# Norm phases that accumulate three projections chunk by chunk, and phases handed over without a meeting of all engines

## Chip, cores and metric

One core of one Trainium2 chip. The metric is the device time of one launch in microseconds (us), here the median of three runs; below, TensorE, VectorE, ScalarE, GpSimd and SyncE are the core's five engines. TensorE multiplies, the three in the middle work elementwise, SyncE only issues the DMA transfers.

## What is computed

One inference step of a trunk of two layers with a final norm. There are 1088 tokens (1024 of a new stream, 64 of a running one), 1024 features, all in fp32. In each layer:

```
mod = silu(c) @ ada_w + ada_b                 # shift, scale, gate of 1024 each, for two kinds of token
h = rmsnorm(x, norm_w) * (1.0 + scale) + shift
proj = h @ w_in                               # q, k, v, z of retention; q, k, v, f, z of fox;
                                              # q, k, v, a, b, z of delta; merge gates
logf = log_sigmoid(ff + fox_f_bias)           # fox: cumulated over the tokens, subtracted in the scores
g = -exp(gdn_a_log) * softplus(ga + gdn_dt_bias);  beta = sigmoid(gb)
o_r = retention(rotary(q), rotary(k), v)      # 4 heads, chunks of 64
o_f = softmax(q k + fcum_q - fcum_k) v        # fox: 8 heads, causal
o_g = gated_delta_rule(l2norm(q), l2norm(k), v, g, beta)   # 4 heads, chunks of 64
br = [rmsnorm(o_r)*silu(z), o_f*silu(z), rmsnorm(o_g)*silu(z)] @ w_branch
x = x + gate * (sum(br * sigmoid(merge gates)) @ w_out)
```

The columns called ff, ga and gb (16 of them in all) are "the gates" of this document. Beside the two outputs of the trunk the step returns the new states of all three branches.

## The kernel before

**Layout.** Features lie on the 128 partitions in eight chunks (`KC`), tokens along the free dimension in three segments of 364, 364 and 360 (`SEGS`). A full fp32 product is made of three fp32r products, high by high, high by low and low by high (`three`, L251 to L256); so h and every block of weights (1024 x 128) exist as a high and a low part. SyncE loads blocks ahead into six raw slots. GpSimd splits each with a cast and a subtraction (`split_block`, L304 to L311). Two split blocks fit in `sb_w_split`. Of h, ScalarE rounds the high part.

**Phases.** The launch is a row of 25 phases: per layer the norm, two retention groups, four fox groups, four delta groups and the merge; then the final norm. Each phase is a program block of its own with one instruction list per engine. At its end `barrier()` (L226) lets all engines meet and clears all semaphores of phases, so that each phase counts from zero; only the counters of loaded and split weight blocks run through the launch.

**Fillers.** Inside a phase TensorE's list is written out by hand. Between the steps of a recurrence or of scores it turns the projections of that group: `blocks` yields one "turn" at a time, which is one chunk of one segment, three matmuls, some 0.5 us; a block has 24 turns. `turns(fill, n)` takes n of them, and the numbers (`front_turns`, the 4 and 8 in retention, 25 at the start of fox) are what covers the other engines' work at that place. A block's last turn releases a PSUM bank to ScalarE, which copies it out.

**The norm phase** (`norm_phase`, L381). x comes in four transfers. ScalarE squares a chunk, TensorE adds the squares over partitions with a matrix of ones (L479), ScalarE takes logarithm and exponential (L518, L521) for the inverse root. Then VectorE multiplies all eight chunks of x with it (L588). Chunk by chunk, ScalarE scales with 1 + scale times the norm's weight, adds the shift and rounds (L550, the high part of h); VectorE forms the difference to the rounded one (L607) and it or ScalarE (L616, L537) the low part. TensorE takes the gates' block as chunks appear: segment 0 over all chunks, then segments 1 and 2. Query and key of retention's first group follow as whole blocks. VectorE turns the gates' rows into logf, g and beta with two scans along the tokens (L645, L647), and SyncE stores them for the later phases. In layer 0 the modulation of a pair of chunks is first computed: TensorE multiplies c with blocks of ada_w (L365), ScalarE copies the row (L527), TensorE turns it into columns (L372), VectorE adds the bias (L378).

**Retention, fox, delta.** Retention starts with five half-swaps for the rotary (L721), projects V for nine bank entries, and waits for the rotated q and k (L745 scores of pairs, L755 transposes). Fox starts with 25 turns and ScalarE's copies of q and k (L1149); the mask that its scores need is prepared by GpSimd (L1060) from a row that SyncE broadcasts. Delta starts with 24 turns, sums of squares for k and q (L335) with ScalarE's logarithms behind them (L1573), and then the products between keys (L1417, L1424).

## Time and profile before

| | |
|---|---|
| median of 3 runs | 3165.54 us (3164.61 to 3170.79) |
| the profiled execution | 3164.03 us |
| its span | 3162.3 us |
| mean granted clock of TensorE | 0.978 |
| TensorE busy | 2948.4 us, 93% |
| VectorE, ScalarE, GpSimd busy | 1106.3, 1014.3, 801.0 us (35%, 32%, 25%) |
| moved by DMA | 269.39 MB, 85 GB/s on average |

The span runs from the first to the last instruction that the profiler recorded. The page cuts it into 40 slices of 79 us and gives each the busy tenths of an engine:

```profile
PE   5999999999999999999959999999999999999996
DVE  3312233233433433155143212343334433422632
PEclk7999999999999999999969999999999999999998
```

PE is TensorE's matmuls, DVE is VectorE, PEclk is the clock that TensorE was granted, in tenths of the full one. Slice 1 holds layer 0's norm, slice 21 layer 1's, slice 40 the final one. In the views of waits an engine with a small q behind it (PEq) is its sequencer.

### The profile page before, as it was taken

To read this page: it belongs to the slowest core of one execution; us is meant where nothing else is said; L and a number is where in the kernel's file an instruction comes from. 1 tells how busy PE (TensorE), PEld (TensorE's weight loads), DVE (VectorE), ACT (ScalarE), POOL (GpSimd) and SP (SyncE) were. 2 spreads that over 40 slices of the span, in tenths; PEclk is the share of its full clock that TensorE was granted. 3 is DMA by queue.
4 is the path that set the end of the run, shared out by engine and by line. 5 is a ranking of instruction groups with operands and counts; after the bars stand their busy time and mean duration, and the time that the engine had idled before them with its cause. 6 is when DMAs were issued, how large, how long until landed. Compare 5 with 4: busy or idle time off the path is not lost. (4 is left out here: it accounts for less than half of the span.)

```text
span 3162.3 us, 55678 instructions
## 1 busy us (share of the span) xinstructions
PE 2948.4 (93%) x24012; PEld 2686.5 (85%) x24012; DVE 1106.3 (35%) x2568; ACT 1014.3 (32%) x1822; POOL 801.0 (25%) x520
## 2 busy tenths in 40 slices
PE   5999999999999999999959999999999999999996
PEld 3988888888898898999948888888888898899995
DVE  3312233233433433155143212343334433422632
ACT  4121423323434544222041214233325534531201
POOL 0221212212313323332212122212213313333320
PEclk7999999999999999999969999999999999999998
DMA  5111223223212211253222112212212211123323
GB/s 217 61 55 49 105 93 116 105 87 115 74 54 56 60 47 56 92 178 101 92 104 68 69 36 90 88 44 90 84 43 57 66 47 56 60 86 142 129 98 142
DMA packets 109956, 269.39 MB, mean 85 GB/s; under 512 B 38992, under 2 KB 45264, under 8 KB 108688
## 3 DMA queue, kind: packets, MB, share of 16 engines
q1 hardware_dynamic: 109712, 265.83, 24.8%
q8 instruction: 190, 3.11, 0.4%
q14 instruction: 54, 0.44, 0.1%
HBM read 208.20 MB, written 57.60 MB: 84 GB/s over the span
## 5 line engine op out<-in xcount | busy, mean ns | idle before, releaser
L254 PE MATMUL ps<-sb_h_split,sb_w_split 128*128 128x364 f32 (+1 forms) x3312 | 1180.7, 356 | 76.8 <-PEq L227 29.6
L256 PE MATMUL ps<-sb_h_split,sb_w_split 128*128 128x364 f32 (+1 forms) x3312 | 1092.7, 330 | 0.1
L255 PE MATMUL ps<-sb_h_split,sb_w_split 128*128 128x364 f32 (+1 forms) x3312 | 1092.6, 330 | 0.0
L254 PEld LDWEIGHTS ps<-sb_h_split,sb_w_split 128*128 128x128 f32 x3312 | 629.8, 190 | 145.4 <-issue 90.0
L308 POOL CAST sb_w_split<-sb_w_raw 128x1024 fp32r<-128x1024 f32 x154 | 166.4, 1081 | 1957.5 <-PE ps L256 1614.0
L255 PEld LDWEIGHTS ps<-sb_h_split,sb_w_split 128*128 128x128 f32 x3312 | 630.3, 190 | 6.4
L256 PEld LDWEIGHTS ps<-sb_h_split,sb_w_split 128*128 128x128 f32 x3312 | 627.4, 189 | 0.4 <-issue 0.4
L310 POOL TENSOR_TENSOR sb_w_split<-sb_w_raw,sb_w_split 128x1024 fp32r<-128x1024 f32 x154 | 370.5, 2406 | 12.3
L1230 DVE COPY sb_fox<-ps 128x512 f32<-128x512 f32 (+3 forms) x208 | 109.0, 541 | 290.4 <-PE ps L1112 289.9
L296 ACT ACTIVATE sb_raw_qk<-ps 128x364 f32<-128x364 f32 (+2 forms) x176 | 64.5, 393 | 347.0 <-PE ps L256 347.0
L1171 ACT ACTIVATE sb_fox<-sb_fox 128x128 f32<-128x128 f32 (+5 forms) x144 | 111.2, 773 | 98.2 <-DVE sb_fox L1208 98.0
L290 ACT ACTIVATE sb_fox<-ps 128x364 f32<-128x364 f32 (+1 forms) x96 | 45.5, 474 | 300.8 <-PE ps L256 300.8
L255 PE MATMUL ps<-sb_h_split,sb_wb_split 128*128 128x364 f32 (+1 forms) x384 | 125.9, 328 | 0.0
L256 PE MATMUL ps<-sb_h_split,sb_wb_split 128*128 128x364 f32 (+1 forms) x384 | 125.6, 327 | 0.0
L254 PE MATMUL ps<-sb_h_split,sb_wb_split 128*128 128x364 f32 (+1 forms) x384 | 125.4, 327 | 0.0
L1112 PE MATMUL ps<-sb_masks,sb_fox 128*128 128x128 f32 (+1 forms) x656 | 105.8, 268 | 0.0
L1202 DVE CUSTOM_DVE_ANT_0 sb_fox<-ps,sb_fox 128x128 f32<-128x128 f32 x144 | 39.9, 277 | 170.3 <-PE ps L1078 126.4
L1112 PEld LDWEIGHTS ps<-sb_masks,sb_fox 128*128 128x128 f32 (+1 forms) x656 | 80.0, 139 | 14.8 <-issue 7.4
L1078 PE MATMUL ps<-sb_fox 64*128 64x512 f32 (+3 forms) x448 | 88.8, 503 | 0.0
L1198 DVE CUSTOM_DVE_ANT_0 sb_fox<-ps,sb_fox 128x256 f32<-128x256 f32 (+7 forms) x128 | 86.3, 674 | 0.0
L1123 PE MATMUL ps<-sb_fox 128*64 128x128 f32 (+2 forms) x1312 | 84.6, 272 | 1.7 <-DVE sb_fox L1230 1.5
L1123 PEld LDWEIGHTS ps<-sb_fox 128*64 128x64 f32 (+1 forms) x1312 | 68.0, 136 | 19.5 <-issue 11.1
(263 smaller groups left out, 4332.0 us busy)
## 6 DMA issues: line engine op xcount, KB each, us to landing
sb_w_raw<-in_wblk SPq DMA_DIRECT2D x154, 512.0 KB, 5.5
sb_ada_fox<-in_adaw SPq DMA_DIRECT2D x32, 512.0 KB, 4.3
sb_raw_qk<-scratch_gate SPq DMA_DIRECT2D x24, 544.0 KB, 3.7
sb_fox<-scratch_fcum SPq DMA_DIRECT2D x8, 1600.0 KB, 7.2
sb_w_raw<-in_wbr SPq DMA_DIRECT2D x48, 256.0 KB, 4.2
scratch_gate<-sb_fox SPq DMA_DIRECT2D x16, 544.0 KB
scratch_gate<-sb_delta SPq DMA_DIRECT2D x16, 544.0 KB
sb_h_split<-scratch_o SPq DMA_DIRECT2D x16, 544.0 KB, 10.5
```

The source lines that it names most:

```text
L254: pe.matmul(out, w_hi, x_hi, start=first, stop=False)
L255: pe.matmul(out, w_hi, x_lo, start=False, stop=False)
L256: return pe.matmul(out, w_lo, x_hi, start=False, stop=last)
L296: ins = act.activation(buf[:, u:u + w], ps[:, first_bank + e % banks, c:c + w], ACT.Copy)
L308: pool.tensor_copy(ws[:, to, 0], wraw[:, slot]).then_inc(split_hi, 1)
L310: pool.tensor_tensor(ws[:, to, 1], wraw[:, slot], ws[:, to, 0].bitcast(F32), ALU.subtract)\
L1078: mm = pe.matmul(ps[0:rows, 2 * h + a // 512, 0:w], qT[64 * h:64 * h + 64, P * t:P * t + rows], kT[64 * h:64 * h + 64, lo + a:lo + a + w], ...
L1112: mm = pe.transpose(ps[0:w, b, P * j:P * j + rows], lg[0:rows, h, (c + j) * P:(c + j) * P + w], ident[0:rows, 0:rows])
L1123: pe.matmul(ps[64 * h:64 * h + 64, b, 0:rows], V[0:w, vt, 64 * h:64 * h + 64], PT[0:w, h, P * c:P * c + rows], start=(c == 0), stop=(c == ...
L1171: act.activation(lg[0:rows, h, 0:n], lg[0:rows, h, 0:n], ACT.Exp, bias=mx[0:rows, s, 2:3], accum_out=mx[0:rows, s, 3:4])\
L1198: dve.tensor_tensor_reduce(out=lg[0:rows, h, 0:n], in0=src[:, 0:n], in1=fk[0:rows, h, lo:lo + n], scale=0.125, scalar=-3e38, op0=ALU.subtr ...
L1230: ins = dve.tensor_copy(dst[:, 0:full, 0:rows], src[:, 0:full, 0:rows])
```

## The change

**Handing over.** The semaphores of phases exist twice, as two sets; phases use them in turn, so a phase needs no cleared counters at its start. All phases stand in one program block. Each engine ends a phase with `leave`, which raises its own counter `done[...]`. ScalarE, VectorE, GpSimd and SyncE begin the next with `enter`: they wait for the other four counters. GpSimd then clears the set of the phase before. TensorE doesn't wait there; it waits for ScalarE alone after eight turns (fox, delta), or before the fourth half-swap (retention's second groups), and at the end of a phase for the copies of its own banks.

```
+        def enter(eng, me, nr):
+            if nr >= 2:
+                eng.wait_ge(sets_cleared, nr - 1)
+            if nr >= 1 and me != "pe":
+                for who in done:
+                    if who != me:
+                        eng.wait_ge(done[who], nr)
+            if nr >= 1 and me == "pool":
+                eng.sem_clear(clears[(nr - 1) % 2])
+                eng.sem_inc(sets_cleared, 1)
+        def leave(eng, me):
+            if me == "pe":
+                eng.sem_inc(done[me], 1)
+            else:
+                eng.drain().then_inc(done[me], 1)
...
-        def barrier():
-            nc.multi_engine_barrier(list(nc.engines), sems_to_clear=clear)
...
+        both = [phases_of(half) for half in range(2)]
+        with nc.Block() as block:
+            for nr, (p, what) in enumerate(order):
+                with ExitStack() as ph:
+                    both[nr % 2][p](block, *what, ph, nr)
```

**The norm.** The gates' weights get a buffer of their own. Gates, query and (in layer 1) two of key's three segments are accumulated side by side in all eight PSUM banks, chunk by chunk; the rest of key follows. In layer 1 the factors 1 + scale times weight are formed at the start and GpSimd multiplies them into x while the squares are summed. VectorE normalises a chunk and forms the low part in one operation. In layer 0 the modulation's products and turns stand between the chunks.

```
+                    def scale_x(k):
+                        pool.wait_ge(squares, k + 1)
+                        for c, (a, w) in enumerate(KINDS):
+                            ins = pool.tensor_scalar(x[:, k, a:a + w], x[:, k, a:a + w], scw[:, k, c:c + 1], None,
+                                                     ALU.mult)
+                        ins.then_inc(merged, 1)
+                    if not first_layer:
+                        pool.wait_ge(scaled, 2)
+                        for k in range(4):
+                            scale_x(k)
+                    split_block(pool, L, 0, wx)
+                    if not first_layer:
+                        for k in range(4, KC):
+                            scale_x(k)
                     split_block(pool, L, 1)
...
+                    def products(k):
+                        if first_layer:
+                            pe.wait_ge(*((level_x, k // 2 + 1) if k % 2 else (h_ready, k // 2 + 1)))
+                        else:
+                            pe.wait_ge(h_ready, k + 1)
+                        for what, s in early:
+                            if k == 0 and s == 0:
+                                await_split(pe, L, what)
+                            product(what, s, k)
...
+                    for k in range(KC):
+                        products(k)
+                        if first_layer and k % 2 == 0 and k < 6:
+                            turn_mods(k // 2 + 1)
+                        if first_layer and k in (1, 3):
+                            mods(k // 2 + 2)
...
+                        normalise(0)
+                        for k in range(KC):
+                            if k + 1 < KC:
+                                normalise(k + 1)
+                            dve.wait_ge(h_hi, k + 1)
+                            for c, (a, w) in enumerate(KINDS):
+                                ins = dve.scalar_tensor_tensor(hs[:, 1, k, a:a + w], x[:, k, a:a + w],
+                                                               modT[:, L, k, c:c + 1],
+                                                               hs[:, 0, k, a:a + w].bitcast(F32),
+                                                               ALU.add, ALU.subtract)
+                            ins.then_inc(h_ready, 1)
```

In the gates' tail, two memsets go to GpSimd, a copy and a scaling to ScalarE, ScalarE's copies of query and key (in layer 1 all six, in layer 0 three) come before its part of the tail, and the scan for g stands before the one for the cumulated logf, whose row is now stored last.

**Fillers.** The split of a retention group's second block moves into the phase before. Retention's 4 turns after each pair of scores go, and the three gaps of 8 turns become 12; in first groups the sixth half-swap stands behind V's fourth entry. In delta the three sums for q are cut in two, with four turns before the last, and ScalarE takes one bank entry earlier. Fox of layer 0 gets 8 turns before its modulation rows.

```
-            front_turns = [24, 4, 10, 2, 4]
+            front_turns = [24, 12, 12, 2, 4]
...
-                    turns(fill, front_turns[0])
+                    turns(fill, 8)
+                    pe.wait_ge(done["act"], nr)
+                    turns(fill, front_turns[0] - 8)
                     pe.wait_ge(squares, 1)
                     sum_features(pe, ring, 0, sq[1])
                     turns(fill, front_turns[1])
                     pe.wait_ge(squares, 2)
-                    sum_features(pe, ring, 3, sq[0])
-                    turns(fill, front_turns[2])
+                    sum_features(pe, ring, 3, sq[0], range(2))
+                    turns(fill, 4)
+                    sum_features(pe, ring, 3, sq[0], range(2, 3))
+                    turns(fill, front_turns[2] - 4)
```

**How rows move on the engines.** The first place is TensorE in layer 1's norm, behind the last sum of squares. `sb_w_split` is the pair of split weight blocks, `sb_h_split` is h. Before:

```order
L479 MATMUL ps<-sb_norm_layer1,sb_masks 128x360
L254 MATMUL ps<-sb_h_split,sb_w_split 128x364 [waits h_ready,roots,split_ready]
L255 MATMUL ps<-sb_h_split,sb_w_split 128x364
L256 MATMUL ps<-sb_h_split,sb_w_split 128x364
L254 MATMUL ps<-sb_h_split,sb_w_split 128x364 [waits level_x]
L255 MATMUL ps<-sb_h_split,sb_w_split 128x364
L256 MATMUL ps<-sb_h_split,sb_w_split 128x364
L254 MATMUL ps<-sb_h_split,sb_w_split 128x364 [waits h_ready]
```

Each wait for a chunk has three matmuls behind it. At the same place now, with `sb_w_gates1` the gates' own buffer (rows left out where they repeat):

```order
L276 MATMUL ps<-sb_h_split,sb_w_gates1 128x364 [waits split_ready,h_ready_0,roots_0]
L277 MATMUL ps<-sb_h_split,sb_w_gates1 128x364
L278 MATMUL ps<-sb_h_split,sb_w_gates1 128x364
...
L276 MATMUL ps<-sb_h_split,sb_w_split 128x364 [waits split_ready]
...
L276 MATMUL ps<-sb_h_split,sb_w_split 128x360
...
L276 MATMUL ps<-sb_h_split,sb_w_split 128x364 [waits split_ready]
...
L276 MATMUL ps<-sb_h_split,sb_w_gates1 128x364 [waits h_ready_0]
```

Between one wait for a chunk and the next stand 24 matmuls: nine for the gates, nine for query, six for key. Behind the first wait of a chunk TensorE also waits for two more splits, once.

The second place is GpSimd in the same norm. Before, it split two blocks there at its phase's start. Now its rows begin so (an ISA row is the clearing of a set, or a wait):

```order
L174 ISA [waits done_act,done_pe,done_dve,done_sp,sets_cleared]
L502 MEMSET sb_norm_layer1 96x1152
L504 MEMSET sb_norm_layer1 96x9 [waits cleared_0]
...
L510 TENSOR_SCALAR sb_norm_layer1<-sb_norm_layer1 128x1024 [waits squares_0,scaled_0]
L510 TENSOR_SCALAR sb_norm_layer1<-sb_norm_layer1 128x64
...
L331 CAST sb_w_gates1<-sb_w_raw 128x1024 [waits slot_loaded_4]
L333 TENSOR_TENSOR sb_w_gates1<-sb_w_raw,sb_w_gates1 128x1024 [waits split_hi]
L510 TENSOR_SCALAR sb_norm_layer1<-sb_norm_layer1 128x1024 [waits squares_0]
```

Four scalings stand ahead of the gates' split and four behind it, and the splits of query and key come after those.

The third place is TensorE in the first retention group, where the rotated q and k are first needed. `sb_ret0` holds them. Before:

```order
L256 MATMUL ps<-sb_w_split,sb_h_split 128x256
L745 MATMUL ps<-sb_masks,sb_ret0 128x128 [waits dve_took,normed]
L745 MATMUL ps<-sb_masks,sb_ret0 128x128 x3
L254 MATMUL ps<-sb_h_split,sb_w_split 128x364 [waits evacuated,split_ready]
L255 MATMUL ps<-sb_h_split,sb_w_split 128x364
L256 MATMUL ps<-sb_h_split,sb_w_split 128x364
```

Now:

```order
L278 MATMUL ps<-sb_w_split,sb_h_split 128x256
L884 MATMUL ps<-sb_masks,sb_ret0 128x128 [waits dve_took_1,normed_1]
L884 MATMUL ps<-sb_masks,sb_ret0 128x128 x3
...
L884 MATMUL ps<-sb_masks,sb_ret0 128x128 [waits dve_took_1]
L893 MATMUL ps<-sb_ret0 128x128 [waits dve_took_1]
L893 MATMUL ps<-sb_ret0 128x128 x7
L276 MATMUL ps<-sb_h_split,sb_w_split 128x364 [waits evacuated_1,split_ready]
```

The transposes of all q and k pieces stand together, with the first products behind them, ahead of the third weight block's first turn (`split_ready`). Before, that turn came after the first four transposes.

## Rows read from the trace of the kernel before

**Rows 1.** The page, part 1: busy us, share, instructions of each engine.

```profile
PE 2948.4 (93%) x24012; PEld 2686.5 (85%) x24012; DVE 1106.3 (35%) x2568; ACT 1014.3 (32%) x1822; POOL 801.0 (25%) x520
```

**Rows 2.** TensorE's waits: what waited, for whom, us in total, times, longest.

```profile
PE ps L254 <- PEq L227: 29.6, 18, 1.7
PE ps L479 <- ACT sb_norm_layer L515: 29.5, 2, 17.5
PE ps L254 <- DVE sb_h_split L616: 18.2, 1, 18.2
PE ps L254 <- ACT sb_h_split L537: 14.6, 5, 3.6
...
PE ps L254 <- POOL sb_w_split L310: 12.6, 4, 3.1
...
PE ps L335 <- ACT sb_delta L1573: 14.1, 8, 1.8
...
PE ps L1097 <- DVE sb_fox L1242: 7.2, 8, 1.7
...
PE ps L1424 <- DVE sb_delta L1719: 6.9, 16, 0.7
```

**Rows 3.** Windows: start:end, us, busy PE, PEld, DVE, ACT, POOL, PEclk, DMA share, GB/s.

```profile
90.00:108.00 18.00, 18.00 (x110) 18.00 (x109) 15.31 (x11) 6.41 (x10) 6.32 (x3) 1.00 0.14 37
1604.60:1644.00 39.40, 8.93 (x22) 5.69 (x22) 26.13 (x41) 21.31 (x30) 0.00 (x0) 0.55 0.08 31
1644.00:1681.30 37.30, 35.24 (x196) 34.97 (x196) 20.29 (x19) 8.95 (x13) 10.61 (x5) 0.92 0.07 18
```

**Rows 4.** Timeline, layer 1's norm: start, us, engine, line, tiles, count, idle before.

```profile
1597.17 2.36 POOL L310 TENSOR_TENSOR sb_w_split<-sb_w_raw,sb_w_split 128x1024 fp32r<-128x1024 f32 x1
...
1608.54 9.70 DVE L588 TENSOR_TENSOR sb_norm_layer<-sb_norm_layer 128x1088 f32<-128x1088 f32 x8 [27.95 <-ACT sb_norm_layer L521]
...
1618.56 3.04 ACT L550 ACTIVATE sb_h_split<-sb_norm_layer,sb_modT 128x1024 fp32r<-128x1024 f32 x4 [10.05 <-DVE sb_norm_layer L601]
...
1620.24 1.48 DVE L607 SCALAR_TENSOR_TENSOR sb_norm_layer<-sb_norm_layer,sb_h_split 128x1024 f32<-128x1024 f32 x2 [1.71 <-ACT sb_h_split L550]
...
1656.47 3.40 POOL L310 TENSOR_TENSOR sb_w_split<-sb_w_raw,sb_w_split 128x1024 fp32r<-128x1024 f32 x1
```

**Rows 5.** Timeline, the gates' tail and the retention group behind it.

```profile
1655.33 0.59 DVE L624 TENSOR_SCALAR sb_norm_layer<-ps,sb_norm_layer 96x360 f32<-96x360 f32 x1 [3.41 <-PE ps L256]
...
1671.30 4.63 DVE L647 TENSOR_TENSOR_SCAN sb_norm_layer<-sb_norm_layer 4x1152 f32<-4x1152 f32 x1
...
1681.29 3.90 PE L721 MATMUL ps<-sb_raw_qk,sb_masks 128*128 128x512 f32 x10 [2.06 <-PEq L227]
...
1687.39 1.42 DVE L895 TENSOR_TENSOR sb_ret<-ps,sb_ret 128x512 f32<-128x512 f32 x3 [5.38 <-DMA sb_ret<-in_sret]
...
1711.37 1.04 POOL L308 CAST sb_w_split<-sb_w_raw 128x1024 fp32r<-128x1024 f32 x1 [26.64 <-PE ps L256]
```

**Rows 6.** Timeline, layer 0's norm: its first low part, and the next phase's start.

```profile
51.81 0.92 DVE L616 TENSOR_SCALAR sb_h_split<-sb_norm_layer,sb_modT 128x1024 fp32r<-128x1024 f32 x2
...
111.22 1.96 PE L721 MATMUL ps<-sb_raw_qk,sb_masks 128*128 128x512 f32 x4 [1.64 <-PEq L227]
```

**Rows 7.** Timeline, the starts of two fox groups.

```profile
351.46 2.30 ACT L1149 ACTIVATE sb_fox<-sb_raw_qk 128x1024 f32<-128x1024 f32 x4 [1.05 <-PEq L227]
...
482.62 0.29 DVE L1202 CUSTOM_DVE_ANT_0 sb_fox<-ps,sb_fox 128x128 f32<-128x128 f32 x1 [21.78 <-POOL sb_fox L1060]
```

**Rows 8.** Timeline, the end of a delta group and the start of the next.

```profile
934.37 0.33 SPq L1380 DMA_DIRECT2D scratch_o<-sb_delta  x1
...
940.21 0.32 SPq L1354 DMA_DIRECT2D sb_delta<-scratch_g  x1
...
958.65 2.83 ACT L1573 ACTIVATE sb_delta<-ps,sb_consts 128x364 f32<-128x364 f32 x6
```

**Rows 9.** The page's DMA issues: KB of each, median us from issue to landing.

```profile
scratch_x<-sb_raw_qk SPq DMA_DIRECT2D x12, 544.0 KB, 2.7
```

More of the change, by code:

```diff
@@ L272, in await_split @@
-        def await_split(eng, L, b):
-            eng.wait_ge(split_ready, L * N_BLOCKS + b + 1)
-        def blocks(pe, L, todo, first_bank, banks):
-            for e, b in todo:
-                await_split(pe, L, b)
-                yield from project(pe, e, first_bank, banks, (b + 1) % 2)
-        def turns(gen, n):
-            for _ in range(n):
-                next(gen, None)
-        def take(act, e, first_bank, banks, dst, func=ACT.Copy):
-            w = dst.shape[-1]
-            act.wait_ge(proj_done, e + 1)
-            act.activation(dst, ps[0:dst.shape[0], first_bank + e % banks, 0:w], func).then_inc(evacuated, 1)
@@ L1637, in _ @@
                     act.wait_ge(stored, 96)
-                    took = 2
+                    kept(2)
+                    took = 3
                     for i in range(6):
```

1023 lines of the change are left out of this document (565 added, 458 removed).

## The prediction, written before the changed kernel was run

> **What bounds the kernel now.** I read the views in this order. The page's first part says that TensorE is busy 93% of the span [rows 1]: the kernel is a stream of matmuls, and a change can only win where that stream stands still. The list of TensorE's waits says where it does [rows 2]. Nothing in it is large. 29.6 us are the meetings of all engines before 18 of the phases (waits on the sequencer, some 1.6 us each), and four more like them stand before retention's swaps, 2.06 us at layer 1's first [rows 5]. About 30 us stand before the sums of squares, and 33 us between the chunks of h (18.2 and 14.6), nearly all in the second layer's norm. The rest repeats once per phase: 1.8 us before the second half of a delta group's sums, 0.4 us twice before its products, 3.1 us before a retention group's third block, 0.7 to 1.7 us in a fox group. The stretches show the norm of layer 1: in the 39.4 us from 1604.6 the engine works 8.9 us, at a mean granted clock of 0.55, between its two levels of 1.2 and 2.4 GHz, while at full clock it takes 110 matmuls in 18 us, 0.165 us each [rows 3]. The timeline there says why: VectorE first scales all eight chunks (9.70 us), then each chunk passes ScalarE and VectorE, and TensorE starts 18.2 after its sums, at 1622.8 [rows 2, 4].
>
> **Part 1, norm of layer 1.** Now GpSimd multiplies x by its column factor under the squares, and VectorE has one product (9.70 / 8 = 1.21 us) and one difference (1.48) per chunk instead of three passes. The inverse root is still there at 1608.5. Then product 1.2, ScalarE's high part 1.5 (3.04 for two), difference 1.5, handings 0.1: the first chunk at 1612.8 against 1622.8 [rows 4]. VectorE delivers a chunk every 2.7 us. TensorE asks for 24 matmuls per chunk, 4.0 us at full clock, so it becomes the bound, with 216 matmuls (24 x 8 and the last key segment's 24): 35.6 us. The clock is charged as it stands after 1644: 0.92 over 37.3 us [rows 3], which is 6 us at the lower level and costs 3 us of work. Sum: 1612.8 + 38.6 = 1651.4.
> GpSimd's scaling has no row. Its one-input cast of 1024 takes 1.04 us, its two-input pass 2.36 [rows 4]; those are my two ends, and I take the cast as the nearer (one tensor in, one out). The factors need small parameters, which land behind x and before the first weight block; that one's second pass starts at 1597.2 [rows 4], so I put them near 1595. So four scalings to 1600, a split (3.4), four more to 1608, two splits to 1615. Key's weights are the last of these and TensorE wants them at 1618 (gate and query products at half clock, 5.5 us): covered. At 2.36 the splits end near 1626 and 7 us are lost.
> VectorE now has two SBUF operands in every pass, beside GpSimd. In the trace a split's second pass takes 3.40 beside such work, 2.36 alone [rows 4]. I charge 2.5 us for this: TensorE ends near 1654. In place of the next phase's first matmul at 1681.3 [rows 5] it comes at 1654.5; with half a microsecond from the earlier start of the phase, the gain is 27.
> The Trainium skill, "SBUF — State Buffer", section "SBUF: two separate sides", says that GpSimd and a VectorE operation with two SBUF inputs take a shared port pair as an exclusive lock and the loser blocks. By that the 11 us of GpSimd left after 1604 would be added whole to VectorE's 21.6: last chunk at 1641, still before TensorE wants it (near 1644), but the first chunks 3 to 5 us later, and the sum would be 3104 to 3106 instead of 3104.
>
> **Part 2, what follows that norm.** The gates' tail took 20.5 us, from the last gate row at 1655.3 to the scan's end at 1675.9 [rows 5], under 24 us of query and key products. Now only 39 matmuls (6.4 us) follow the last gate. ScalarE takes the query and key first (+3.5), the cumulated row is stored last (+2.7, the landing of a store [rows 9]), handing 0.5: the other engines enter retention 27.2 after the gates, 20.8 after TensorE's end. TensorE goes on alone with the swaps (3.9) and V for three bank entries (17.3). VectorE needs its entry, 6.0 us of parameter landing and 8.3 of rotary [rows 5]: q and k stand at 35.1, but V ends at 30.0 (1711.3 less 1681.3 [rows 5]). So a new wait of 5 us takes the place of the 3.1 before the third block: loss 1.9. In layer 0 key comes wholly after the gates (72 matmuls, 12 us, and query's 1.5), and this wait stays away; a split beside VectorE's scans may cost 1.5.
>
> **Part 3, norm of layer 0.** Here the chunks come in pairs, each pair behind a modulation that TensorE itself turns. Before, the turns did not stand behind products. Now 18 products of the chunk before stand ahead of it, and after each turn TensorE waits some 3.6 us for the next odd chunk: 0.65 for VectorE's small operations, 1.5 twice for ScalarE (3.04 for two [rows 4]). One round is 3.0 + 1.9 + 3.0 + 1.1 of work, 3.6 of waiting, and 1.7 for a dip of the clock: 14.3. The first chunk is out at 52.7 [rows 6]; its 18 products at the lower level (0.33 each, 5.9) end near 59.3 with the handings. Three rounds lead to about 102 with the last chunks, then the key's 12.0: 114.2, plus 0.6 until its banks are out, against 111.2 [rows 6]. Loss 3.6. At half clock throughout a round is 20.1 and the loss 17; with no dip at all it is a gain of 2. The row for the bad end is [rows 3]: 8.9 us of work in 39.4 left the clock at 0.55; here work is three quarters of a round, so I stay near the good end.
>
> **Part 4, the phases without meetings.** TensorE no longer waits for others at a phase's start, only after 8 turns (4 us) for ScalarE. But the others start as late as ever: ScalarE's last copy ends 0.5 after the last matmul, then 1.05 to the next phase's first work [rows 7]; half of that may stay, so they enter 1.0 after TensorE rather than 0.
> Fox: VectorE's first operation ends a wait on GpSimd [rows 7], which stands behind the landing of a broadcast, so TensorE waits longer at its third turn. What remains is the shorter handing, 0.6, for four groups, and 1.1 for the four that have 0.5 of slack: 6.8.
> Delta: the 1.63 at ten starts (eight groups, two merges) is 16.3. Twelve turns for four, four in the middle of the sums and twelve for ten cover the 1.77: it comes from ScalarE at 958.65, 18.4 after its phase's start at 940.2 [rows 8], and TensorE is there after 40 turns and five pairs of sums, 23.1. But ten turns (5 us) fewer stand at the end. The last store is issued at 934.4 and lands 2.7 later [rows 8, 9], TensorE now ends near 933.6 on that scale: the others enter the next group 3.7 late, so of the 2.6 of waits per group 1.9 come back in six of eight. Gain 9.9, less 0.6 in the merges.
> Retention, second groups: 1.6 for the start, and 5 transposes and 8 products now lie in the 3.1: 1.7. Two groups: 6.6. First group of layer 0: 0.2. The final norm's start: 0.5.
>
> **Sum.** 27.5 (part 1 with 0.5 for its start) - 1.9 - 3.6 + 6.8 + 25.6 + 6.6 + 0.2 + 0.5 = 61.7 us. The profiled execution is 3164.0, 1.5 under the median of three: 3102.3 there, 3104 as a median.
>
> **Rivals.**
> *Idle only moves.* If all starts are bound by the other engines, the 40 us of parts 4 come to the shorter handing, 22 x 0.6 = 13, and the norms give 22: 3130. For it: fox, where I find this already. Against: delta and merge, whose first need of others lies 12 us in [rows 8].
> *A slow norm.* GpSimd at its two-input price (7) and layer 0 at half clock (13 more): 3124. For it the clock row [rows 3]; against it the share of work.
> The Trainium skill, "TensorE: Matmul & The Clock Gate", section "HAM oscillation — how this bites in real kernels", says that gaps bring the slow clock back each time round; the trace agrees where chunks came one by one, 0.55. It speaks for this rival.
> *All of it works.* No waits come back in delta, retention or layer 0: 11 + 5 + 4 more, 3086.
> *Slower.* The new handing (a drain on each engine, four waits, GpSimd's clearing of a set) costs more than a meeting. It decides from 1.6 + 61.7 / 22 = 4.4 us per handing; at 6 us it adds 22 x 1.6 = 35 to before: 3200. Against it: one meeting with all of this in it takes 1.05 after ScalarE's last copy [rows 7].
>
> **Chances.** Forecast 0.58 (own range 3096 to 3113), idle moves 0.14, slow norm 0.14, all works 0.11, slower 0.03. The range 3088 to 3130 leaves out half of the best case, the far side of the two bad ones and the slower case. Faster by over 0.2% (6 us, about what a measurement tells from none) 0.95, within 0.2% 0.02, slower 0.03.
>
> **What would show it.** TensorE's waits on the sequencer nearly gone; its first product in layer 1's norm near 1613 less what was won before, that phase some 27 us shorter and at full clock from its second chunk; in layer 0 three waits of 3 to 4 us behind the turned modulations; one new wait of some 5 us before the transposes of layer 1's first retention group; in fox the wait for V's copy longer, not shorter; GpSimd's scaling near 1.1 us. I am wrong if that scaling takes over 2 us, or if delta's phases don't shrink by 2 to 4 us each.

## The result and the profile after

The kernel got slower. Its median is 3198.97 us (3196.28 to 3203.78, 4 runs) against 3165.07 us for the kernel before (3162.83 to 3170.79), a ratio of 1.0106 with a 95% interval of 1.0087 to 1.0125. The forecast was 3104 us, within 3088 and 3130. The profiled execution has a span of 3201.8 us against 3162.3.

Part 1 of the page after answers to [rows 1]:

```profile
PE 2966.2 (93%) x24012; PEld 2709.2 (85%) x24012; DVE 1147.6 (36%) x2540; ACT 1013.2 (32%) x1820; POOL 847.0 (26%) x544
```

The same 24012 matmuls take 17.8 us more, and the mean granted clock is 0.973 against 0.978; VectorE has 28 instructions fewer and is busy 41 us more. Both are odd for a change that should only close gaps. TensorE's waits after answer to [rows 2] (waiting line, releaser, us in total, times, longest):

```profile
PE ps L276 <- ACT sb_delta L312: 38.7, 16, 3.4
PE ps L542 <- ACT sb_norm_layer L616: 27.7, 2, 17.5
PE ps L276 <- POOL sb_w_split L333: 24.6, 5, 18.1
...
PE ps L276 <- DVE sb_h_split L754: 12.1, 1, 12.1
PE ps L1250 <- DVE sb_fox L1402: 12.0, 8, 2.6
...
PE ps L276 <- ACT sb_delta L318: 11.2, 7, 1.7
PE ps L276 <- ACT sb_h_split L638: 10.8, 3, 3.6
```

The 29.6 us of meetings are gone. In their place stand 50 us of waits in delta, for ScalarE's copies out of the fillers' banks (L312 and L318), and one wait of 18.1 us for a split of weights in layer 1's norm. In fox the wait for V's copy (L1402) grew from 7.2 to 12.0, as the prediction had said.

To place the loss, take each phase from its first matmul to the next phase's first. First the windows of the kernel before, then those of the kernel after; the three lines are layer 0's four delta groups, layer 1's four, and layer 1's norm (start:end, us, busy PE, PEld, DVE, ACT, POOL, PEclk, DMA share, GB/s).

```profile
826.90:1283.10 456.20, 427.29 (x5169) 397.83 (x5169) 179.68 (x360) 220.12 (x437) 139.99 (x89) 1.00 0.20 56
2368.10:2824.20 456.10, 427.21 (x5169) 397.93 (x5169) 179.74 (x360) 220.12 (x437) 138.64 (x89) 1.00 0.19 56
1587.80:1681.30 93.50, 60.95 (x265) 50.66 (x265) 46.42 (x59) 39.14 (x51) 17.34 (x9) 0.76 0.19 69
```

```profile
819.50:1302.10 482.60, 438.10 (x5171) 407.83 (x5170) 200.02 (x359) 219.98 (x436) 141.18 (x88) 0.98 0.18 52
2380.80:2866.60 485.80, 440.64 (x5170) 409.90 (x5170) 200.29 (x359) 219.99 (x436) 140.53 (x88) 0.97 0.18 52
1605.20:1697.00 91.80, 58.56 (x265) 50.26 (x265) 37.10 (x32) 27.00 (x39) 52.89 (x27) 0.78 0.19 74
```

The delta groups took 912.3 us and take 968.4: 56 us lost. Of these, 24 are the same matmuls at a lower clock (427.29 + 427.21 us busy against 438.10 + 440.64, PEclk 1.00 against 0.98 and 0.97) and 32 are idle time of TensorE. VectorE is busy 41 us more in them. The norm of layer 1 gains 1.7 where 27 was forecast. Everything else together gained 15 us.

Inside one delta group after, from the timelines of VectorE and TensorE:

```profile
942.86 13.12 DVE L1883 SCALAR_TENSOR_TENSOR sb_delta<-sb_raw_qk,sb_delta_small,sb_delta 128x1024 f32<-128x1024 f32 x12 [1.61 <-ACT sb_delta L1723]
951.12 2.10 PE L359 MATMUL ps<-sb_delta,sb_masks 128*128 128x364 f32 x6 [1.33 <-ACT sb_delta L1733]
958.74 0.43 PE L276 MATMUL ps<-sb_h_split,sb_w_split 128*128 128x364 f32 x1 [1.54 <-ACT sb_delta L318]
968.26 0.43 PE L276 MATMUL ps<-sb_h_split,sb_w_split 128*128 128x360 f32 x1 [3.43 <-ACT sb_delta L312]
```

Before, the twelve passes of k's and q's convolution (six of 1024 elements, six of 64) took 9.03 us:

```profile
943.47 9.03 DVE L1706 SCALAR_TENSOR_TENSOR sb_delta<-sb_raw_qk,sb_delta_small,sb_delta 128x1024 f32<-128x1024 f32 x12 [1.53 <-ACT sb_delta L1549]
```

GpSimd's rows say what stood beside these passes. Before, its first split ends at 943.8 and its second begins at 952.5, as the twelfth pass ends:

```profile
941.35 2.41 POOL L310 TENSOR_TENSOR sb_w_split<-sb_w_raw,sb_w_split 128x1024 fp32r<-128x1024 f32 x1
952.52 1.04 POOL L308 CAST sb_w_split<-sb_w_raw 128x1024 fp32r<-128x1024 f32 x1 [3.19 <-PE ps L256]
```

After, the first split overlaps the first pass, and the second falls on the passes of q. The last row here is three of the twelve passes (64, 1024 and 64 elements), which take 4.58 us in place of 1.8:

```profile
942.05 2.40 POOL L333 TENSOR_TENSOR sb_w_split<-sb_w_raw,sb_w_split 128x1024 fp32r<-128x1024 f32 x1
949.98 1.08 POOL L331 CAST sb_w_split<-sb_w_raw 128x1024 fp32r<-128x1024 f32 x1
951.14 3.24 POOL L333 TENSOR_TENSOR sb_w_split<-sb_w_raw,sb_w_split 128x1024 fp32r<-128x1024 f32 x1
949.89 4.58 DVE L1883 SCALAR_TENSOR_TENSOR sb_delta<-sb_raw_qk,sb_delta_small,sb_delta 128x64 f32<-128x64 f32 x3
```

So two suspects: TensorE stops in the middle of fillers for a bank (theory F), and VectorE's convolution has become slower by 4.1 us per group beside GpSimd (theory P). Delta's fillers use two PSUM banks (`B0, NB = 5, 2`), eight turns to a bank. The 33rd turn needs the bank that ScalarE empties with the third copy of v (L318), the 41st the one that it empties behind its exponential (L312). A third stop of 1.4 us for L312 comes some 16 us later in each group.

### The profile page after: what moved, and what is told of

The parts are those of the page before. It is cut to its first block and busy times, and to the rows that moved or that the text cites. A ratio compares the mean times of both kernels' runs of the same rounds, so it can differ in the third digit from the quotient of the medians.

```text
span 3201.8 us, 55475 instructions
## 1 busy us (share of the span) xinstructions
PE 2966.2 (93%) x24012; PEld 2709.2 (85%) x24012; DVE 1147.6 (36%) x2540; ACT 1013.2 (32%) x1820; POOL 847.0 (26%) x544
## 5 line engine op out<-in xcount | busy, mean ns | idle before, releaser
L318 ACT ACTIVATE sb_raw_qk<-ps 128x364 f32<-128x364 f32 (+2 forms) x176 | 64.6, 394 | 353.4 <-PE ps L278 353.3
L312 ACT ACTIVATE sb_fox<-ps 128x364 f32<-128x364 f32 (+1 forms) x96 | 45.5, 474 | 298.5 <-PE ps L278 298.5
L1883 DVE SCALAR_TENSOR_TENSOR sb_delta<-sb_raw_qk,sb_delta_small,sb_delta 128x1024 f32<-128x1024 f32 x96 | 105.1, 1142 | 14.0 <-ACT sb_delta L1723 12.9
## 6 DMA issues: line engine op xcount, KB each, us to landing
sb_h_split<-scratch_o SPq DMA_DIRECT2D x16, 544.0 KB, 10.7
```

What stands on the lines that cost most here:

```text
L1883: ins = dve.scalar_tensor_tensor(c[:, b:b + w], u[:, a + j:a + j + w], cw[:, 4 * x + j:4 * x + j + 1], c[:, b:b + w], ALU.mult, ALU.add)
```

## The experiments

The experiments ran in three sessions, and the kernel before ran in each: its median was 3168.2 us beside the first to the fourth, 3165.05 beside the fifth to the eighth, and 3168.09 beside the rest. Each ratio is to the kernel before of the same session. A difference to the changed kernel (3198.97, with 3165.07 before) therefore carries some 3 us.

**The fillers taken back** in the changed kernel. The cut leaves out the third part, ScalarE's bank entry, which goes back too.

```
-                front_turns = [24, 12, 12, 2, 4]
+                front_turns = [24, 4, 10, 2, 4]
...
-                    sum_features(pe, ring, 3, sq[0], range(2))
-                    turns(fill, 4)
-                    sum_features(pe, ring, 3, sq[0], range(2, 3))
-                    turns(fill, front_turns[2] - 4)
+                    sum_features(pe, ring, 3, sq[0])
+                    turns(fill, front_turns[2])
```

> The changed kernel with delta's fillers as before: turns 24, 4, 10, 2, 4, the three sums for q together, ScalarE's third bank entry where it was. All else stays changed. Theory F (banks): in the delta groups the fillers now run into their ring of two PSUM banks: a bank is filled in eight turns, and ScalarE empties it only at its written place, behind its logarithms and a table load. TensorE waits 1.5, 3.4 and 1.4 us there per group, and the clock falls behind these waits. With the old numbers those three waits go and one of about 4 us before the sums' second half comes back: idle per group from 11.1 to about 8, the clock stays up, delta phases shrink by 4 us each: 3199 - 32 = 3167, at least under 3180. Theory P (the shared port of VectorE and GpSimd): what makes delta late is that VectorE's convolution passes stretch beside GpSimd's splits, 4.1 us per group; the fillers only show it. Then the wait moves to the logarithms and the time stays within 8 us: 3191 to 3199.

Measured: 3164.55 us, ratio to the kernel before 0.9989 (0.9978 to 1.0). That is 34 us under the changed kernel, as theory F expected. The delta groups fall from 968.4 to 930.8:

```profile
820.00:1284.30 464.30, 434.03 (x5169) 405.72 (x5168) 193.63 (x360) 220.92 (x436) 142.56 (x88) 0.97 0.20 55
2361.00:2827.50 466.50, 437.86 (x5171) 407.86 (x5170) 193.63 (x360) 220.92 (x436) 143.03 (x88) 0.96 0.19 55
```

They are still 18.5 us over before. Nearly all of that is the clock, which I had expected to stay up: the matmuls take 871.9 us against 854.5, and the idle time (58.9 us against 57.8) is back where it was. The bank waits have turned into these, 3.0 us and up to 2.2 us in each group:

```profile
PE ps L359 <- ACT sb_delta L1731: 24.2, 8, 3.0
PE ps L359 <- ACT sb_delta L1745: 14.5, 8, 2.2
```

TensorE now waits for the squares of q, which come behind the end of the convolution, and for the logarithms behind its sums. What remains points at theory P; the next experiment tests it.

**GpSimd's second split held back.**

```
                     pool.wait_ge(proj_done, 3)
+                    pool.wait_ge(conv_done, 2)
                     split_block(pool, L, first + 2)
```

> The changed kernel with one wait added: in a delta group GpSimd starts the second block's split only when VectorE has done the convolutions of k and q. Theory P: the passes that took 1.94 and 2.40 us beside that split fall back to 1.28 and 0.28, so q's squares come 2.8 us earlier per group, 8 x 2.8 = 22 and some of the clock's dips: 3172 to 3180. Theory F: the banks hold TensorE up behind ScalarE's chain, which starts from these squares too, so part of it is to be seen, but the 3.4 us behind the logarithms stay as they are, since that chain hangs on TensorE's own last sum: 3185 to 3195.

Measured: 3181.13 us, 1.0039 (1.0025 to 1.0053): 18 us won. That is 1 us above theory P's range and 4 under theory F's. The ten runs spread from 3168 to 3191, and the profiled one is the fastest, so its rows are used for single instructions and waits and not for the price. VectorE's passes in the same group:

```profile
939.30 10.35 DVE L1884 SCALAR_TENSOR_TENSOR sb_delta<-sb_raw_qk,sb_delta_small,sb_delta 128x1024 f32<-128x1024 f32 x12 [1.61 <-ACT sb_delta L1724]
```

Twelve passes take 10.35 us in place of 13.12: the 2.8 expected. The first pass still stands beside the first split (2.69 us, the others of 1024 elements 1.28). The wait for L312 is unchanged (38.6 us in 16 times), so both causes are there side by side.

**The norm's splits ahead of the last scalings.**

```
                     split_block(pool, L, 0, wx)
+                    split_block(pool, L, 1)
+                    split_block(pool, L, 2)
                     if not first_layer:
                         for k in range(4, KC):
                             scale_x(k)
-                    split_block(pool, L, 1)
-                    split_block(pool, L, 2)
```

> The changed kernel, in layer 1's norm GpSimd splits query's and key's block right behind the gates' one, before the last four scalings of x. Theory: what failed in that norm is GpSimd's price, 3.3 us for a scaled chunk (2.85 and 0.44) where 1.04 to 2.36 was taken, so that query's block came 18 us late. With the order changed the waits of 18.1 and 2.4 us go, the chunks come every 3.3 to 4 us instead: that phase from 91.7 to about 72, the kernel 3199 - 20 = 3179. Rival: VectorE's passes beside GpSimd's splits and scalings stretch so far that the chunks bound TensorE: under 10 us won, 3190 or more.

Measured: 3176.64 us, 1.0026 (1.0017 to 1.0036), 22 us won; the phase takes 70.8 us against 91.8, its clock is 0.86 against 0.78:

```profile
1600.10:1670.90 70.80, 56.36 (x264) 48.67 (x264) 36.89 (x32) 26.94 (x39) 50.09 (x27) 0.86 0.25 96
```

GpSimd's rows in the changed kernel say what the order had cost. Four scalings take 14.10 us, then the gates' split, four more 18.97, and only at 1651.5 does query's split begin, while TensorE was through with the first chunk's gate products at 1637.9 (its wait of 18.05 us ended at 1655.97):

```profile
1614.19 14.10 POOL L510 TENSOR_SCALAR sb_norm_layer<-sb_norm_layer 128x1024 f32<-128x1024 f32 x8 [13.79 <-DVE sb_norm_layer L700]
1628.24 1.03 POOL L331 CAST sb_w_gates<-sb_w_raw 128x1024 fp32r<-128x1024 f32 x1
1629.36 3.26 POOL L333 TENSOR_TENSOR sb_w_gates<-sb_w_raw,sb_w_gates 128x1024 fp32r<-128x1024 f32 x1
1632.60 18.97 POOL L510 TENSOR_SCALAR sb_norm_layer<-sb_norm_layer 128x1024 f32<-128x1024 f32 x8
1651.53 1.03 POOL L331 CAST sb_w_split<-sb_w_raw 128x1024 fp32r<-128x1024 f32 x1
```

**Only the fillers, in the kernel before.** The diff of the first experiment the other way round, with meetings, norm and all else as they were.

> The kernel before, with meetings and its norm, and only the new numbers of fillers in delta (24, 12, 12, 2, 4, the sums for q cut in two, the third bank entry earlier). Theory F: the wait of 3.4 us behind the last sum comes here too (exponential with its table load, 1.28 + 1.11, and the copy 0.46, all behind TensorE's own sum), in place of the 1.8 and 0.7 before: 8 x 1 to 8 x 3 longer, 3173 to 3190. Theory P: the fillers are harmless without the late convolution, as the prediction had it: 3150 to 3165.

Measured: 3233.03 us, 1.0208 (1.0191 to 1.0226). The fillers alone cost 65 us, far outside the ranges of both theories (up to 3190 and up to 3165), and the prediction had put a gain on them. Waits, and the delta groups of the two layers:

```profile
PE ps L254 <- PEq L227: 46.6, 18, 3.8
PE ps L254 <- ACT sb_delta L290: 38.8, 16, 3.4
```

```profile
829.10:1313.90 484.80, 437.18 (x5168) 408.27 (x5169) 187.62 (x360) 221.14 (x437) 138.88 (x89) 0.97 0.19 53
2398.60:2890.00 491.40, 440.54 (x5168) 411.11 (x5169) 187.98 (x360) 221.17 (x437) 139.39 (x89) 0.97 0.18 52
```

The wait of 3.4 us for the bank is there as expected (with a second of 1.4). Two prices had been left out. The turns drawn to the front are missing at the end, so TensorE is there early and the meetings grow from 29.6 us to 46.6 in all, up to 3.8 each. And the clock: 23 us of the loss are the same matmuls at 0.97. In the changed kernel the meetings' share can't show, since TensorE doesn't wait there. In the delta groups the fillers cost 41 us of idle time and 23 of clock here, and 31 and 7 there (the changed kernel less the first experiment).

**All three repairs.**

> The edits of the first three experiments together: delta's fillers as before, its second split held back until k and q are convolved, and the norm's splits ahead of the last four scalings. The causes add up: fillers 34, norm 22, and with the fillers back the stretched convolution passes still stand in the chain that TensorE waits for, 2.8 us a group, 22: 3199 - 78 = 3121, within 3115 and 3135. Delta phases then near 113, under the 114.0 of before. If the second edit only moves a wait, as the banks would have it, the sum is 3143.

Measured: 3125.91 us, 0.9871 (0.9855 to 0.9886). The sum of causes was 3121; it holds within 5 us (with the 18 us that the second experiment measured in place of 22 it would be 3125), and the version that would have spoken against theory P (3143) is out. The delta groups take 909.6 us, 2.7 less than before the change, where the prediction had 23: 13 for the eight starts and 9.9 for the fillers, which are taken back here. TensorE's idle time in them fell by 10.7 us (47.1 against 57.8), near the 13, but the same matmuls took 8.0 us more (862.5 against 854.5), at a granted clock of 0.98 and 0.99 where it was 1.00. So the starts gave nearly what was forecast, and the clock took most of it back; no run separates why it stayed lower.

```profile
819.10:1275.50 456.40, 432.59 (x5171) 404.54 (x5170) 182.01 (x360) 220.37 (x436) 140.45 (x88) 0.98 0.20 56
2338.70:2791.90 453.20, 429.92 (x5169) 401.90 (x5169) 181.97 (x360) 220.24 (x436) 139.43 (x88) 0.99 0.20 57
```

**The next group's split moved to the group's end.** `split_block(pool, L, first + DELTA_N + 1)` after `proj_done` 15, and the one at the start only in the first group.

> The three repairs, and GpSimd splits the next delta group's second block at the end of a group (three of four per layer) instead of at its start, where it stands beside VectorE's first convolution pass. Port theory: that pass falls from 2.7 to 1.28 us in six groups, their squares of k come 1.4 us earlier, 6 x 1.4 = 8 us: 8 under the three repairs alone. Rival: TensorE's first wait there is set by the entry of the other engines, and VectorE has to wait for its parameters or for ScalarE's first tap anyway: within 2 us of the three repairs.

Measured: 3134.24 us, 0.9894 (0.9878 to 0.991): 8 us slower than the three repairs, not 8 faster, and so outside both expectations. The first pass did fall to 1.28 us. But VectorE's entry into the group shows the price, with the repairs alone and then with the moved split:

```profile
1046.24 0.24 DVE L1866 COPY sb_raw_qk<-sb_delta_small 128x3 f32<-128x3 f32 x2 [5.02 <-ACTq L182]
```

```profile
1046.17 2.38 POOL L333 TENSOR_TENSOR sb_w_split<-sb_w_raw,sb_w_split 128x1024 fp32r<-128x1024 f32 x1
1048.81 0.24 DVE L1870 COPY sb_raw_qk<-sb_delta_small 128x3 f32<-128x3 f32 x2 [8.11 <-POOLq L182]
```

The wait grows from 5.0 to 8.1 us, and its releaser is now GpSimd's sequencer: a split that stands ahead of `leave` holds up all engines that wait for GpSimd's counter.

**TensorE waits at a phase's start too.** In `enter`, `if nr >= 1 and me != "pe":` becomes `if nr >= 1:`.

> The three repairs, but TensorE too waits at a phase's start for all other engines' counters, so that it never runs ahead; two sets, drains and clearing stay. What running ahead is worth is read from it. Theory: 1.0 us per start in fox, 1 in retention's second groups and 1.5 in the merges, and in delta almost nothing, since each microsecond that TensorE gains at the start it waits at the sums: in all 10 to 20 us slower than the three repairs, delta phases longer by under 1 us. Rival, the prediction's account: 1.6 us at each of 22 starts less a third that comes back, 25 or more slower, delta phases longer by 1.5 us.

Measured: 3162.35 us, 0.9985 (0.9976 to 0.9995), 36 us slower than the three repairs. In total this looks like the rival, but the places are others. The waits and the phases:

```profile
PE ps L858 <- SPq L182: 28.3, 2, 17.7
...
PE ps L276 <- ACTq L182: 17.2, 18, 1.0
```

```profile
838.40:1293.70 455.30, 429.06 (x5169) 401.02 (x5169) 181.82 (x359) 220.87 (x437) 140.96 (x88) 0.99 0.20 56
2369.90:2827.20 457.30, 429.51 (x5168) 400.98 (x5169) 181.84 (x359) 220.82 (x437) 140.17 (x88) 0.99 0.20 56
```

28.3 us are the two starts behind the norms, where the gates' tail runs on after TensorE's last product. At the starts of retention's second groups TensorE waits 3.8 us each for GpSimd (7.6 us in 2 times). The other 18 starts, in fox, delta and merge, are 1.0 us at most, and the delta groups take 912.6 us against 909.6. Told by phases, of the 36 us 26 lie in the two norms (9.2 and 16.7), 6 in retention and 4 in all the rest. Running ahead pays behind the norms, somewhat in retention, and nearly nowhere else. I had expected 10 to 20 us because I had left the norms' tails out.

**No scaling on GpSimd.** The three repairs; in layer 1's norm `scale_x` goes, ScalarE applies `scale=scw[:, k, c:c + 1]` as in layer 0, and VectorE has a third pass. The cut shows VectorE's part alone.

```
-                                ins = dve.scalar_tensor_tensor(hs[:, 1, k, a:a + w], x[:, k, a:a + w],
-                                                               modT[:, L, k, c:c + 1],
-                                                               hs[:, 0, k, a:a + w].bitcast(F32),
-                                                               ALU.add, ALU.subtract)
+                                ins = dve.scalar_tensor_tensor(x[:, k, a:a + w], x[:, k, a:a + w],
+                                                               scw[:, k, c:c + 1],
+                                                               hs[:, 0, k, a:a + w].bitcast(F32),
+                                                               ALU.mult, ALU.subtract)
+                            link(ins)
+                            for c, (a, w) in enumerate(KINDS):
+                                ins = dve.tensor_scalar(hs[:, 1, k, a:a + w], x[:, k, a:a + w],
+                                                        modT[:, L, k, c:c + 1], None, ALU.add)
```

> The three repairs, and GpSimd scales nothing in layer 1's norm: ScalarE applies the factor when it rounds, and VectorE has three passes a chunk (1.2, 1.5 and 0.9 us) interleaved chunk by chunk, TensorE's order as in the change. Theory: the scaling on GpSimd earned nothing, because 3.6 us a chunk on VectorE is still under the 4.0 that TensorE needs, and without GpSimd beside it the passes don't stretch: first products 5 us behind the inverse root instead of 5 or more, the phase 66 to 70 us against 70.8 of the reordered splits. Rival: the third pass binds VectorE, chunks come at over 4.2 us, and the phase is 2 or more longer than 70.8.

Measured: 3119.91 us, 0.9848 (0.9833 to 0.9864). The norm takes 66.6 us (73.5 in the three repairs), GpSimd is busy 16.07 us in it and not 51.05:

```profile
1578.40:1645.00 66.60, 56.41 (x264) 48.90 (x264) 31.69 (x48) 28.31 (x39) 16.07 (x11) 0.88 0.27 102
```

Against before (93.5 us) the norm is 26.9 shorter, so what wins in it is the new order, chunk by chunk, of TensorE's products and VectorE's passes; no run separates these two. Moving work to GpSimd cost 7 us even with the splits in front. That 26.9 meets the 27 of the forecast is luck in part, since the forecast rested on the scaling that is gone here.

**Fillers within the banks**, on top of the kernel of the eighth experiment: 24, 8, 8, 2, 4, with the sums for q divided, so that no 41st turn stands before the products.

> The kernel of the eighth experiment, with delta's fillers 24, 8, 8, 2, 4 and the sums for q cut in two with four turns between; at most 40 turns stand before the products, since the 41st needs the bank that ScalarE empties behind its exponential. Theory F (banks): the waits of 0.8 and 2.2 us at the sums are filled, the waits of 3.4 and 1.4 us of the changed kernel don't come, idle per delta group from 5.8 to 3.5, 8 x 2 us: 3104, within 3098 and 3112. Rival (whatever stands before the sums delays ScalarE's logarithms and comes back at the products or at the group's end): within 6 us of 3120.

Measured: 3119.13 us, 0.9843 (0.9826 to 0.9859), no difference to the eighth (0.9848), where theory F had expected 16 us. The rival is right. The waits at the sums are gone, and this one came:

```profile
PE ps L1588 <- DVE sb_delta L1894: 24.4, 11, 2.8
```

**The same numbers in the kernel before.**

> The kernel before with the same fillers 24, 8, 8, 2, 4 and the divided sums, meetings as they were. Against the fourth experiment it differs by eight turns that stand after the products and not before the 41st turn's bank is free. Theory F: the wait of 3.4 us behind the last sum goes and most of the 1.8 us too: 8 x 1 to 2 us faster than before, 3150 to 3158, where 24, 12, 12 was 65 slower. Rival (turns at the start are missing at the end, whatever the banks): slower than before, 3175 or more.

Measured: 3172.33 us, 1.0014 (1.0004 to 1.0025). It falls between the two expectations, nearer to the rival's. Against the fourth experiment 61 us are won, but not by the bank alone. The eight turns also stand at the group's end again, and the meetings are back at 29.4 us from 46.6, 17 of the 61. Of the delta groups' own 55 us (921.6 against 976.2), 35 are idle time and 19 the clock (858.3 against 877.7 us busy). Against before nothing is won, rather 4 us lost: no wait for L290 among the large ones, and again a wait before the products.

```profile
PE ps L1425 <- DVE sb_delta L1722: 22.2, 12, 2.4
```

**GpSimd's first split beside the convolution, in the kernel before.**

```
+                    pool.wait_ge(tap_done, 1)
                     split_block(pool, L, first + 1)
```

> The kernel before with one wait: in a delta group GpSimd starts its first split when ScalarE has made the first tap, so that it stands beside VectorE's first two convolution passes. Port theory: passes of 1.28 become up to 2.7 beside the cast and subtraction (3.4 us), the convolutions end 1.4 to 3 us later and TensorE's waits at the sums grow by as much: 8 x 1.5 to 8 x 3, 3178 to 3190. Rival (only the changed kernel's own order stretches them): 3162 to 3170.

Measured: 3202.12 us, 1.0113 (1.0093 to 1.0132), 34 us slower by one wait in an idle engine. Theory P had the direction right and too small a price (3178 to 3190), as it left the clock out. Here both splits fall on the passes, so that more is lost than the 4.1 us of the changed kernel. The twelve passes take 14.80 us, and TensorE waits up to 3.3 us a group for what follows them:

```profile
946.05 14.80 DVE L1707 SCALAR_TENSOR_TENSOR sb_delta<-sb_raw_qk,sb_delta_small,sb_delta 128x1024 f32<-128x1024 f32 x12 [1.53 <-ACT sb_delta L1550]
PE ps L335 <- ACT sb_delta L1560: 26.0, 8, 3.3
```

```profile
825.30:1298.40 473.10, 439.68 (x5168) 406.56 (x5169) 199.42 (x360) 221.27 (x437) 144.11 (x89) 0.96 0.19 54
```

A group grows by 4.3 us for 5.8 us in VectorE, and 12 of a layer's 17 us are the clock (439.68 against 427.29).

## Why the prediction was wrong

The forecast had a gain of 61.7 us and the profiled spans show a loss of 39.5. Of the 101 us between them, 79 are delta (22.9 of gain forecast, 56.1 of loss measured) and 26 are the norm of layer 1 (27.5 and 1.7); the rest came out 4 us better than forecast. Both signs of being wrong that the prediction names appeared: the scaling took over 2 us, and the delta groups grew by 7 us each.

**Part 4, delta: the step that failed most.** It said that twelve turns for four and four in the middle of the sums "cover the 1.77", and 9.9 us of gain. I counted turns as time only. A turn also holds a bank: with two banks of eight turns each, the 33rd and the 41st wait for ScalarE at its written place. The second comes behind the logarithm of TensorE's own last sum, a table load and an exponential, and no earlier start helps it: it is 3.4 us in the changed kernel and in the fourth experiment alike. The fillers alone cost 65 us in the kernel before, and within the banks they cost 4 and win nothing (fourth and tenth experiments). The 65 are the bank's waits, the meetings that grew, and the clock; the bank's wait isn't separated from the other two by a run of its own. The likely reason that they win nothing is that ScalarE's chain hangs on the sums, and each turn ahead of a sum delays it; the waits at the sums went and one before the products came (2.8 us, ninth experiment).

**Part 4, the starts.** The prediction counted 1.63 at ten starts, less 1.9 in six of eight groups. (Its own terms, 2.6 in eight groups less 1.9 in six, make 9.4 and not 9.9.) It took VectorE's convolution to be as long as before. GpSimd enters a little after VectorE (its first row is at 940.94, VectorE's at 940.43) and its first split, which before had nearly ended when the first pass began, now stands beside it; TensorE, which runs ahead, finishes the first block earlier against VectorE, and so the second split falls on the passes of q. This is the coupling that was missed: who runs ahead also triggers. It costs 4.1 us per group in VectorE (13.12 against 9.03), shown by the second experiment, which takes 2.8 of them away, and by the last, which makes such an overlap, a larger one, in the kernel before. With the fillers back and the second split held, delta has 2.7 us of gain in eight groups. The fox groups gained 8 us in all and the merges with the final norm 4.5, near the forecast; retention's second groups 1.9 where 6.6 was forecast.

Of this contention I had spoken in the norm alone, where I charged 2.5 us. The trace of before had it in every delta group too: VectorE's product of 128x1088, 1.29 us by itself, took 2.84 beside GpSimd's.

```profile
963.95 1.29 DVE L1719 TENSOR_TENSOR sb_delta<-sb_delta 128x1088 f32<-128x1088 f32 x1 [2.06 <-ACT sb_delta L1623]
966.36 2.84 DVE L1719 TENSOR_TENSOR sb_delta<-sb_delta 128x1088 f32<-128x1088 f32 x1 [1.12 <-ACT sb_delta L1627]
```

The Trainium skill, "SBUF — State Buffer", section "SBUF: two separate sides", says that GpSimd and a VectorE operation with two SBUF inputs take the shared pair of ports as an exclusive lock, and whichever starts first has it for the whole instruction. The trace agrees: a VectorE pass of 64 elements, 0.28 us alone, took 2.40 us beside GpSimd's subtraction (952.06 to 954.46), and the two ended together within 0.1 us. I had applied the page's rule to the one phase that the change rewrites, and it decided in the phases whose instructions stayed the same.

**Part 1, the norm of layer 1: the price of GpSimd's scaling.** The prediction bounded it by 1.04 (a cast) and 2.36 (two inputs) and took the cast. It is 2.85 for the 1024 and 0.44 for the 64 columns where VectorE doesn't work beside it, above both ends; four chunks took 18.97 us beside VectorE. The rest was right: the small parameters landed 15 us after x was issued, as forecast, and TensorE's price of 4.0 us a chunk bound the phase once the splits stood first. The first chunk was late as well: TensorE waited 12.1 us for it behind its sums, against 18.2 before and some 8 forecast. VectorE's first difference took 3.36 us beside GpSimd's split of the gates, and the second 1.27. The lateness is near the 3 to 5 us that the prediction had worked out beside its 2.5. What the scaling held back was above all the splits behind it: their wait was worked out as none at 1.04 and 7 us at 2.36, and it was 18.1. The bound should have been open above, since no row showed a product with a column on GpSimd. That this was the price is shown by the third experiment (22 us for the order of the splits) and the eighth (6 us more without the scaling).

**Parts 2 and 3** held. The norm of layer 0 ends at 115.3 (114.8 forecast), with the three waits of 3.6 us behind the turned modulations. (The bad end of part 3 was summed wrongly: three rounds of 20.1 in place of 14.3 add 17 to the loss of 3.6, which makes 21 and not 17. The slow norm would then be 3128.) The new wait in front of layer 1's first retention scores is 5.1 us (5 forecast). That layer 0's first retention group gains 4.9 and not 0.2 was missed: its start costs 0.9 us less, the third block's wait goes from 3.1 to 1.2, and a fall of the clock to its lower level for 3.4 us (1.7 us of work) doesn't come.

**The rivals.** None had this form. That all works would end at 3084 by its own terms, and not at 3086. "Idle only moves" ended at 3130, since an idle time that moves can't become longer; the waits did come back in delta, as it said, but what lengthened them was outside it. "Slower" was priced by the new handing over, which costs less than a meeting: 1.0 us at most at 18 of the 22 starts in the seventh experiment, against 1.63. Its time, 3200, is the measured one by coincidence.

**The clock** was charged in the norms only. In delta TensorE idles 11 us a group after the change where it was 7, with a single stop of 3.4 us, and the granted clock of those groups falls from 1.00 to 0.97 and 0.98: 24 us, three quarters as much as the added idle time itself. Against the kernel before, the matmuls of the delta groups take longer by such a share in every experiment, from 2.5 us (the ninth) to 25 (the eleventh). The Trainium skill, "TensorE: Matmul & The Clock Gate", section "HAM oscillation — how this bites in real kernels", says that gaps between stretches of matmuls bring the slow level back each time round; the trace agrees, with the lower level at least once in each of the eight delta groups after the change.

## What to carry to other kernels

A filler (work turned in while another engine is busy) is not only time: count what it holds (a bank, a buffer) and in whose written order this comes free, and stop the fillers one before that. An engine that is allowed to run ahead moves every piece of work that its progress triggers; for each of these look for what stands beside it on the other engines, VectorE and GpSimd above all. Where an operation has no row, a bound from similar rows is a guess with an open end, and what is queued behind it should be ordered so that the end can't hurt.

## What the runs showed of the hardware

- GpSimd multiplies 128x1024 fp32 by a column in 2.85 us, more than it needs for a difference of two such tensors (2.36); VectorE's product of two 128x1088 tensors takes 1.2.
- VectorE and GpSimd in each other's way: passes of 1.28 us (1024 elements) became 1.9 to 3.4, those of 0.28 us (64 elements) became 1.1 to 2.4, and GpSimd's subtraction went from 2.40 to 3.2 in delta and 3.4 in the norm (the changed kernel; in delta also the eleventh experiment).
- A stop of 3.4 us in an otherwise busy stretch was followed by a stretch at the lower clock (0.76 over the five us from 970.0 in the changed kernel, after the stop that ended at 968.3).
- With TensorE waiting too, the handing over by counters costs at most 1.0 us at the 18 starts in fox, delta and merge (seventh experiment); the meeting cost 1.63 there.
